# Hybrid encoder block on one core: x loaded in quarters between its weight units, parameter loads on SyncE, and the GLU gate kept in PSUM

## The reference, cut to what matters

```python
hn = rms_norm(h, norm1_g[l])                       # h = [meta tokens; x], 272 x 2048
q, k, v, u, g_na, g_ssm = jnp.split(hn @ w_in[l], IN_SPLITS, axis=-1)
y_na  = neighbourhood_attention(q, k, v, na_rpb[l]) @ w_proj_na[l]
y_ssm = s5_branch(u, ...) @ w_proj_ssm[l]
mixed = sigmoid(g_na) * y_na + sigmoid(g_ssm) * y_ssm
h = h + mixed @ w_out[l]
h = h + conv_gated_ffn(rms_norm(h, norm2_g[l]), w_up[l], conv_w[l], conv_b[l], w_down[l])

# the end of s5_branch, the "GLU":
y = gelu(y)                                        # 1024 wide
return y * sigmoid(y @ w_glu)
```

## Time and profile before

| what | us |
|---|---|
| median of three runs | 1496.82 |
| the profiled execution, its own time | 1495.8 |
| its span in the trace | 1494.0 |
| PE busy | 1463.7 (98%) |
| POOL busy | 1052.0 (70%) |
| ACT busy | 672.0 (45%) |
| DVE busy | 583.0 (39%) |

### The profile page before, as it was taken

The page is one execution under the profiler, slowest core; times in us unless marked ns, Lnnn a source line. Parts: engine busy times, 40 slices in busy tenths (PEclk is TensorE's granted clock), DMA queues, the critical chain, the costliest instruction groups (busy, mean ns, idle before and its releaser), DMA issues.

```text
span 1494.0 us, 30698 instructions
## 1 busy us (share of the span) xinstructions
PE 1463.7 (98%) x11826; PEld 1390.5 (93%) x11826; DVE 583.0 (39%) x1151; ACT 672.0 (45%) x913; POOL 1052.0 (70%) x496
## 2 busy tenths in 40 slices
PE   8999999999899999999999999999999999999997
PEld 7999999998789899999999999999999998888886
DVE  3766888888453434443322222222222222003002
ACT  6446444431354364445454444444444443334333
POOL 5400038873477677898788888888888887888885
PEclk9999999999999999999999999999999999999999
DMA  7897457653576545575565556555555555555553
GB/s 215 291 218 220 141 164 216 194 171 104 133 228 192 173 152 184 172 252 181 176 184 184 182 182 183 182 182 182 182 182 183 183 183 197 189 190 185 189 187 131
DMA packets 247422, 277.14 MB, mean 185 GB/s; under 512 B 26652, under 2 KB 233852, under 8 KB 246700
## 3 DMA queue, kind: packets, MB, share of 16 engines
q1 hardware_dynamic: 232768, 254.84, 56.0%
q10 hardware_dynamic: 14508, 21.09, 4.3%
q0 software_dynamic: 64, 0.07, 0.0%
HBM read 263.32 MB, written 12.39 MB: 185 GB/s over the span
## 4 chain that ended last, share of the span: by engine, by line
PE 81%; DVE 10%; DVEq 2%; issue 2%; ACT 2%; SPq 1%; DMA 1%; ACTq 0%
PE ps L1537 20%; PE ps L1539 20%; PE ps L1538 20%; PE ps L1907 6%; PE ps L1906 5%; PE ps L1905 5%; DVE ps L1065 3%; DVE scan_states L1254 3%; DVEq L1253 2%; DVE t L1065 1%; PE ps L1747 1%; DMA v_tail_ring<-v_scratch 1%; ACT w_hi L520 1%; DVE w_lo L524 1%; DMA w_raw<-in_w_in 0%
## 5 line engine op out<-in xcount | busy, mean ns | idle before, releaser
L524 POOL TENSOR_TENSOR w_lo<-w_raw,w_hi 128x1024 fp32r<-128x1024 f32 x425 | 1022.8, 2412 | 402.6 <-ACT w_hi L520 263.1
L520 ACT ACTIVATE w_hi<-w_raw 128x1024 fp32r<-128x1024 f32 x464 | 490.1, 1060 | 682.9 <-PE ps L1539 508.4
L1537 PE MATMUL ps<-act_hi,w_hi 128*128 128x258 f32 (+2 forms) x2432 | 697.5, 287 | 1.0 <-DVE act_lo L1006 1.0
L1539 PE MATMUL ps<-act_hi,w_lo 128*128 128x258 f32 (+2 forms) x2432 | 693.3, 285 | 0.0
L1538 PE MATMUL ps<-act_lo,w_hi 128*128 128x258 f32 (+2 forms) x2432 | 692.1, 285 | 0.0
L1537 PEld LDWEIGHTS ps<-act_hi,w_hi 128*128 128x128 f32 x2432 | 464.2, 191 | 6.5 <-issue 4.6
L1538 PEld LDWEIGHTS ps<-act_lo,w_hi 128*128 128x128 f32 x2432 | 464.5, 191 | 0.0
L1539 PEld LDWEIGHTS ps<-act_hi,w_lo 128*128 128x128 f32 x2432 | 463.1, 190 | 0.0
L1905 PE MATMUL ps<-w_hi,hidden_hi 128*128 128x512 f32 x352 | 139.2, 395 | 0.0
L1906 PE MATMUL ps<-w_hi,hidden_lo 128*128 128x512 f32 x352 | 139.0, 395 | 0.0
L1907 PE MATMUL ps<-w_lo,hidden_hi 128*128 128x512 f32 x352 | 139.0, 395 | 0.0
(11 more groups left out here) (268 smaller groups left out, 1553.1 us busy)
## 6 DMA issues: line engine op xcount, KB each, us to landing
w_raw<-in_w_up SPq DMA_DIRECT2D x176, 512.0 KB, 3.5
w_raw<-in_w_in SPq DMA_DIRECT2D x128, 512.0 KB, 4.1
w_raw<-in_w_down SPq DMA_DIRECT2D x88, 512.0 KB, 3.8
w_raw<-in_w_out SPq DMA_DIRECT2D x32, 512.0 KB, 3.4
w_raw<-in_w_proj_na SPq DMA_DIRECT2D x16, 512.0 KB, 3.3
w_raw<-in_w_proj_ssm SPq DMA_DIRECT2D x16, 512.0 KB, 3.3
w_raw<-in_w_glu SPq DMA_DIRECT2D x8, 512.0 KB, 3.5
bias_rows<-skew_scratch ACTq DMA_DIRECT2D x24, 128.0 KB
```

Of the source, the lines that this page charges most:

```text
L520: act.activation(slot(whi, k), slot(raw, k), ACT.Copy).then_inc(s_hi, 1)
L524: pool.tensor_tensor(slot(wlo, k), slot(raw, k), slot(whi, k).bitcast(F), ALU.subtract).then_inc(s_lo, 1)
L1537: mm(o, slot(whi, k)[:, cols], xh[:, kt, lo:lo + n], start=kt == 0, stop=False)
L1539: ins = mm(o, slot(wlo, k)[:, cols], xh[:, kt, lo:lo + n], start=False, stop=kt == units * UKT - 1)
```

## The change

Four edits. (1) x is loaded in quarters of 512 columns, each followed by one unit of `w_in`; of the first quarter one piece goes through ACT's queue. (2) The ten parameter loads go to SP, behind unit 3 and ahead of unit 4. (3) PE transposes the gain rows behind the tiles k = 0 to 2, and two idle passes ahead of the first product go. (4) The sigmoid of the GLU is written back to its own PSUM bank, and DVE multiplies from there; ACT no longer waits for the multiplies of the first half before the sigmoids of the second, and PE waits for four multiplies instead of four sigmoids before it writes these banks again.

```diff
-        s_x = [sem(f"x_loaded_{h}") for h in range(2)]
+        s_x = [sem(f"x_quarter_loaded_{q}") for q in range(4)]
...
+        def x_piece(eng, q, n):
+            cs = slice(q * UKT * P, (q + 1) * UKT * P)
+            dst, src = ((xtok[0:N_META, 0, cs], meta[:, cs]), (xtok[N_META:P, 0, cs], x[0, 0:P - N_META, cs]),
+                        (xtok[:, 1, cs], x[0, P - N_META:2 * P - N_META, cs]),
+                        (xtok[0:N_META, 2, cs], x[0, 2 * P - N_META:SEQ, cs]))[n]
+            eng.dma_start(dst, src).then_inc(s_x[q], 16)
...
-            x_load(0)
-            load_in(U_U, 3 * HALF, 0, range(2))
-            x_load(1)
-            load_in(U_U, 3 * HALF, 0, range(2, 8))
+            for q in range(4):
+                for n in (1, 0, 3, 2):
+                    if q or n != 2:
+                        x_piece(sp, q, n)
+                load_in(U_U, 3 * HALF, 0, (q,))
+            for h in range(2):
+                sp.dma_start(rows[:, 0, 64 * h:64 * h + 64], lam_re[0].rearrange("d g n -> (d g) n")).then_inc(s_par, 16)
...
+            load_in(U_U, 3 * HALF, 0, range(4, 8))
...
+            x_piece(act, 0, 2)
             for n, g in enumerate((norm1_g[0], norm2_g[0])):
                 act.dma_start(grow[n * KT:(n + 1) * KT, :], g.rearrange("(k p) -> k p", p=P)).then_inc(s_gain, 16)
-            for h in range(2):
-                act.dma_start(rows[:, 0, 64 * h:64 * h + 64], lam_re[0].rearrange("d g n -> (d g) n")).then_inc(s_par, 16)
...
             def token_square(t, h, nth):
                 n = (P, P, N_META)[t]
-                act.wait_ge(s_x[h], 64)
+                act.wait_ge(s_x[2 * h], 64)
+                act.wait_ge(s_x[2 * h + 1], 64)
...
                 act.wait_ge(s_used, U_GLU + 4 * (q + 1))
-                if q:
-                    act.wait_ge(s_z, 4)
-                else:
+                if q == 0:
                     act.wait_ge(s_g, G_SSM + G_ATT + SEED)
                 for m in range(4):
-                    act.activation(gt[:, m, :], ps[:, GLU_BANKS[4 * q + m], 0:NL], ACT.Sigmoid).then_inc(s_sg, 1)
+                    gate = ps[:, GLU_BANKS[4 * q + m], 0:NL]
+                    act.activation(gate, gate, ACT.Sigmoid).then_inc(s_sg, 1)
...
-                dve.tensor_tensor(mt[:, n % 4, :], yT[:, n, LIVE:L], gt[:, n % 4, :], ALU.mult).then_inc(s_z, 1)
+                dve.tensor_tensor(mt[:, n % 4, :], yT[:, n, LIVE:L], ps[:, GLU_BANKS[n], 0:NL], ALU.mult).then_inc(s_z, 1)
...
-            pe.wait_ge(s_gain, 32)
-            nc.tensor.transpose(ps[:, 7, 0:2 * KT], grow[:, :], ident[0:2 * KT, 0:2 * KT]).then_inc(s_gtp, 1)
...
-                if k % KH == 0:
-                    pe.wait_ge(s_x[k // KH], 64)
+                if k % UKT == 0:
+                    pe.wait_ge(s_x[k // UKT], 64)
...
-            for k in range(6):
+            for k in range(3):
                 x_transposes(k)
-            idle_passes(2)
+            pe.wait_ge(s_gain, 32)
+            nc.tensor.transpose(ps[:, 7, 0:2 * KT], grow[:, :], ident[0:2 * KT, 0:2 * KT]).then_inc(s_gtp, 1)
+            x_transposes(3)
             for q in range(4):
                 for m in range(2):
-                    if q == 0 and m == 1:
-                        x_transposes(6)
-                        x_transposes(7)
-                    if q in (1, 2):
+                    if q < 3:
                         x_transposes(4 * q + 4 + 2 * m)
                         x_transposes(4 * q + 5 + 2 * m)
...
-            pe.wait_ge(s_sg, 4)
+            pe.wait_ge(s_z, 4)
```

More of the change, by code:

```diff
@@ L423, in load_in @@
                     load(first + 8 * i, k, kblock(w_in[0], i * (2 * CB) + (col0 + (k // 4) * CB), k % 4))
-            x_load(0)
-            load_in(U_U, 3 * HALF, 0, range(2))
-            x_load(1)
-            load_in(U_U, 3 * HALF, 0, range(2, 8))
+            for q in range(4):
[5 more added lines that the diff above has]
+                sp.dma_start(rows[:, 0, 64 * h:64 * h + 64], lam_re[0].rearrange("d g n -> (d g) n")).then_inc(s_par, 16)
+                sp.dma_start(rows[:, 1, 64 * h:64 * h + 64], lam_im[0].rearrange("d g n -> (d g) n")).then_inc(s_par, 16)
+            sp.dma_start(lst[:, 0:1], log_step[0].rearrange("d (g a) -> (d g) a", a=1)).then_inc(s_par, 16)
+            sp.dma_start(drow[:, :, :], ssm_d[0].rearrange("(q g c) -> q g c", q=PAIRS, g=2)).then_inc(s_par, 16)
+            for n in range(3):
+                sp.dma_start(crow[n % 2 * FT:(n % 2 + 1) * FT, n // 2, :],
+                              conv_w[0, n].rearrange("(k p) -> k p", p=P)).then_inc(s_par, 16)
+            sp.dma_start(crow[FT:2 * FT, 1, :], conv_b[0].rearrange("(k p) -> k p", p=P)).then_inc(s_par, 16)
+            load_in(U_U, 3 * HALF, 0, range(4, 8))
             with sp.Fori(1, ITERS_IN) as i:
```

## The result

The changed kernel took 1502.35 us (median of 20 runs, 1499.24 to 1507.34), the kernel before beside it 1498.84 (20 runs, 1492.84 to 1502.61): ratio 1.0033, interval 1.0024 to 1.0042. It is slower by 0.33% (the two medians alone would give 0.23%, the two means 0.32%). The time lies in the predicted range (1494.8 to 1503.6), but the likeliest case, no change that could be told, did not come: the whole interval lies above 1. The profiled execution took 1506.25 us, near the top of its 20 runs, so lengths are compared here place by place and not by its span.

The account below looks back on a forecast made before the run. PE, busy 98% of the span, was taken as the bound. Terms -0.5 + 2.9 + 1.4 = +3.8 on the profiled 1495.8 gave 1499.6; with 1.0 for the median, 1500.6 us, range 1494.8 to 1503.6.

Parts of the forecast that it names:

- The GLU, the wait: End of the GLU: three of four `z_lo` held by POOL, PE's wait growing from 2.0 to 4.9 us, +2.9 us.
- Rival B: GLU: the four `z_lo` go through as one from 547.8, without clock loss; 1494.8 us, chance 0.12.
- C: Rival at the GLU: only unit 4 collides, unit 5 comes late; 1497.0 us, chance 0.12.
- The clock term: Behind the GLU wait: at least one stretch at 1.2 GHz, +1.4 us; bounds 0, and +3 with a second.
- The start: Kernel start: first product at 13.65 instead of 14.12 us, from dropping two idle passes; -0.5 us, bounds -1.3 and +1.
- The sum: Whole kernel: -0.5 for start, +2.9 for GLU wait and +1.4 for clock make +3.8 us.
- How the numbers follow: Whole-kernel chances: about 0.3%, 4.5 us, can be told from no change; slower 0.32, faster 0.06, no change 0.62.
- A: The forecast itself, at the GLU: three of four `z_lo` held; 1500.6 us, chance 0.62.
- D: Rival: A, plus unit 4 or a quarter of x late, or a second low stretch; 1502.5 to 1504, chance 0.14.
- Parameters on SP: Start: unit 4's DMA goes out about 2 us later, within 3.7 us of cover, costing nothing.

Follow-up runs that it names:

- the dose: Kernel before plus sigmoid written to PSUM, with zero, one or two of POOL's units let in between the `z_lo`: 1494.78, 1497.88 and 1500.87 us.
- the product in PSUM: Kernel before plus the GLU sigmoid written back to PSUM, and the multiply's product kept there too: 1495.33 us, ratio 0.9977.
- the start alone: Changed kernel with the GLU's sigmoid edit undone, leaving x quarters, parameter loads on SP, later gain rows and no idle passes: 1498.66 us, ratio 1.0002.
- the run with one unit held: Kernel before plus sigmoid written to PSUM, with ACT waiting for the eight `z_lo` only ahead of rounding unit 5: 1497.88 us, ratio 1.0001.
- edit 4 alone: Kernel before with only the GLU edit, sigmoid written back to PSUM and multiplied from there: 1500.87 us, ratio 1.0017.
- holding both units back: Kernel before plus sigmoid written to PSUM, with ACT waiting for the last `z_lo` before rounding unit 4 and those behind it: 1494.78 us, ratio 0.9972.
- PE busy on idle passes: Kernel before plus sigmoid written to PSUM, with PE running 20 idle passes before its first-block wait for `z_lo`: 1500.18 us, ratio 1.0011.

## Why the prediction was wrong

**The GLU, the wait: right.** Forecast 2.3, 2.6, 2.6 and 0.4 us for the `z_lo` and 4.9 for PE's wait; they are 2.18, 2.59 (the pair of 4.69 ends at 555.68, the second begins at 553.10), 2.56 and 0.41, and 4.71. It adds 2.67, forecast 2.9. That POOL's instructions between the `z_lo` are the cause is shown by the dose (0.38, 2.55, 4.71) and by the product in PSUM. Rival B, the four as one, needs only 0.42 for each behind the first; the rows show one between two POOL instructions. C needs unit 5 to come late; it is rounded at 554.02, while POOL still works.

**The clock term: a step that failed, in its size.** Forecast +1.4 for one low stretch, with +3 as the bound for two. The five profiles with the wait of 4.71 have one stretch three times and two twice: 1.5, 1.5, 1.2, 2.6 and 2.6, on average 1.9. I took the second stretch for the exception; it was there in the profiles of the first and the second measurement. Why one or two is not shown.

**The start: the other step that failed, -0.5 that is not there.** The first product did come earlier by about what was forecast: 0.52 in the two first profiles (13.26 against 13.78 in the timeline; the forecast 13.65 started from 14.12, the end of the idle passes). In all it is 12.59 to 13.48 in four profiles, against 13.7 to 14.0 in six with the old start. But the start alone gives 1.0002, between -1.2 and +1.8 us. PE does not lose the lead by waiting: behind the first product, up to 48 us, it stands still only four times, for 0.11 to 0.41 us each, as before, so no unit and no quarter of x is late. What differs in the profiles is the clock. With the old start the clock falls early, here in the run with one unit held (stretches as in the earlier trace rows); its first product is at 13.89:

```profile
7.70:11.10 3.40, 3.08 (x11) 1.68 (x11) 1.72 (x4) 2.63 (x5) 0.00 (x0) 0.50 1.18 314
11.10:14.50 3.40, 3.40 (x15) 2.60 (x15) 2.77 (x7) 2.66 (x5) 2.36 (x1) 0.50 1.01 254
14.50:17.90 3.40, 3.40 (x16) 2.95 (x15) 0.26 (x1) 0.51 (x2) 2.36 (x1) 0.50 1.08 306
```

With the new start it falls at 11.6, equally for three stretches, of which nearly all lies behind the first product:

```profile
8.40:11.60 3.20, 1.18 (x7) 0.68 (x6) 2.30 (x7) 2.29 (x4) 0.84 (x1) 1.00 1.09 301
11.60:14.90 3.30, 2.54 (x10) 2.14 (x11) 2.29 (x7) 2.40 (x4) 2.10 (x2) 0.50 1.09 299
14.90:18.30 3.40, 3.40 (x15) 2.66 (x14) 1.30 (x4) 0.52 (x1) 1.78 (x1) 0.50 1.13 288
18.30:21.80 3.50, 3.50 (x17) 3.00 (x15) 0.69 (x2) 2.71 (x5) 0.00 (x0) 0.50 1.02 286
```

Low clock ahead of the first product costs little, since PE only fills time there; behind it each us costs about half of one. The first ends 4.0 us behind its first product, the second 8.5. Half of those 4.5 us, less the lead of 0.6 at the product (13.26 against 13.89), makes a lag of 1.6 as an estimate; at the convolution's rows, the next fixed place, it is 1.2 (50.70 against 49.48). Of this, 0.17 is a longer gap of PE just ahead of them (1.20 to 1.22 us in all eight profiles with the new start, 1.05 in the six with the old one).

Over all profiles: with the old start (six) the clock falls at 7.7 to 10.4 and is low for 3.8 us on average behind the first product, and the convolution's rows come at 49.3 on average (48.6 to 51.0); with the new start without passes (four) it falls at 10.9 to 11.8, is low for 8.5 behind it, and the rows come at 50.5 (49.3 to 51.6). So the fall of the clock moved later, behind the first product, and the prediction's start term had no clock in it. These are single executions, and the profile of the start alone shows no such lag (49.3); the twelve runs of the start alone show neither a gain nor a loss.

**The sum, and the step from it to the chances.** With these sizes: 0 for the start, 2.7 for the wait, 1.9 for the clock, 4.6 us or 0.31%, where the forecast had 3.8 or 0.25%. The three measurements of the change are 1.0033, 1.0025 and 1.0027, or 4.9, 3.7 and 4.0 us. The mechanism was right and the sum at most a little short. The step that then gave the wrong answer is the bound in "How the numbers follow": +3.8 us was counted as no change because about 0.3%, 4.5 us, was held to be what a measurement can tell. The intervals here reach 0.09 to 0.14% to either side, 1.3 to 2 us, so +3.8 itself would have been told from nothing, and "slower" should have had most of A and of D, not 0.32. Rival D named the second stretch, and two of the three profiles of the change have it, but its price (+5.7 to +7.2) is above all three measurements; A's +3.8 lies nearer. That the time itself, 1502.35, is near D's 1502.5 is chance: the kernel before came out 2.0 us above its first three runs (1498.84 against 1496.82).

**Parameters on SP: right.** Unit 4 landed at about 21.2 (15.3 + 5.9) and was taken at 26.26.

**What stays open.** The parts alone add to 0.0019, the whole is 0.0025 to 0.0033; the intervals allow both that they add and that about 1 us comes on top. The granted clock, averaged over all executions, leaves it open too: the time lost to it is 0.1 us more than before with the start alone and 1.0 with edit 4 alone, but 3.6 and 1.1 in the second and third measurement of the whole. And holding both units back won 4.0 us of the median where the wait shrank by only 1.66 (keeping the product in PSUM 3.5 for 2.04). Averaged over its executions the granted clock was also higher than before (13.4 us lost to it, before 14.9), but no profile shows at which place. Among the versions with edit 4 on the old start, times and places agree: both units held is 6.1 us under edit 4 alone, for 4.33 of wait and 1.5 of clock, and the product in PSUM 5.5, for 4.71 and 1.5. Against the kernel before, each of the three is 1 to 2.5 us faster than its places say, edit 4 alone too (+2.6, by its places 2.67 + 1.5). Where these versions gain that is not known.

## What to carry to other kernels

Before you free an instruction that was held by a shared port, look at what it held back in turn: here four slow multiplies kept ACT, and through it POOL, out of the way of the subtracts that PE waits for. Take the port conflict out of the whole chain to the waiting engine, or delay the other side (one wait on ACT took 6.1 us off edit 4 alone); half a cure moves it nearer to the end. Where a wait of the bounding engine doubles, count the low clock behind it as a term with two sizes, and where the start moves, ask whether the fall of the clock comes ahead of or behind the first real product. And before a small forecast is called "no change", work out from the scatter and the number of runs what the measurement will resolve.

## What the runs showed of the hardware

- DVE with two SBUF inputs and POOL take turns one for one even when DVE has four in its queue: each POOL instruction let in between costs PE 2.17 us.
- A wait of 2.55 us left PE at 2.4 GHz behind it, one of 4.71 brought 3.4 or 6.8 us at 1.2 GHz in all five profiles; at an equal delay of the products, with PE busy on idle passes, none.
- A sigmoid written back to its PSUM bank takes no longer than one written to SBUF: four in 1.19 us, before 1.18.
- Execution times of one kernel scatter by 2 us and more around the median (the kernel before: 1492.84 to 1502.61), and in the profiles the part behind the GLU, 943.3 us of 1494, has almost no share in that.
